# First attention: its dense pieces dealt out in halves, three quarters of the second projection taken into the last steps

## What is computed

```python
h = rmsnorm(x, attn_pre_g)
q_n, kc, vc, ksl, vsl, kwn, vwn, g_n, q_s, k_s, v_s = split(h @ w_in)
k_cmp, v_cmp = compress_kv(kc, ...), compress_kv(vc, ...)
gates = sigmoid(g_n)
# 8 heads: softmax over compressed, selected and window keys, summed by gates
o_nsa = nsa_attention(q_n, k_cmp, v_cmp, ksl, vsl, kwn, vwn, gates)
# 8 heads: softmax over a window of 128 keys, with sinks
o_swa = swa_attention(q_s, k_s, v_s, sinks)
mix = concatenate([o_nsa, o_swa]) @ w_o
x = x + rmsnorm(mix, attn_post_g)
```

## Time and profile before

| | us |
|---|---|
| median of three runs | 1287.24 (1286.85 to 1287.76) |
| the profiled execution | 1286.42 |
| its span, first to last instruction | 1284.5 |
| TensorE busy | 1263.0 |
| VectorE busy | 786.6 |
| ScalarE busy | 647.9 |
| GpSimd busy | 216.9 |

### The profile page before, as it was taken

How to read it: one execution, slowest core, us unless ns; L and a number is a source line. 1 busy time by engine, 2 the same in 40 slices (tenths; PEclk the granted TensorE clock), 3 DMA queues, 4 the chain that set the end, 5 groups by cost and what they waited for, 6 DMA issues and landing times.

```text
span 1284.5 us, 16448 instructions
## 1 busy us (share of the span) xinstructions
PE 1263.0 (98%) x6004; PEld 1045.6 (81%) x6004; DVE 786.6 (61%) x1465; ACT 647.9 (50%) x1261; POOL 216.9 (17%) x234
## 2 busy tenths in 40 slices
PE   9999999999999999999999999999999999999998
PEld 8887888878888888888787777887888888888887
DVE  6689687686645565356788876589644343343334
ACT  6787788554335433233555655586533252332344
POOL 0064555000100011001002101032311030110111
PEclk9998999999999999999999999999999999999999
DMA  7211110423333323332333212432333324233332
GB/s 275 86 50 34 42 41 26 170 82 99 90 100 98 98 90 99 99 96 68 115 91 98 76 56 68 131 112 68 98 99 92 97 75 118 79 115 89 100 90 67
DMA packets 64626, 118.20 MB, mean 92 GB/s; under 512 B 7713, under 2 KB 12193, under 8 KB 64289
## 3 DMA queue, kind: packets, MB, share of 16 engines
q1 hardware_dynamic: 62704, 112.86, 29.3%
q10 hardware_dynamic: 1840, 4.29, 1.1%
HBM read 115.02 MB, written 2.10 MB: 91 GB/s over the span
## 4 chain that ended last, share of the span: by engine, by line
PE 90%; DVE 4%; ACT 2%; issue 2%; DMA 1%; POOL 1%; POOLq 0%; SPq 0%; DVEq 0%; ACTq 0%
PE bank L593 26%; PE bank L595 25%; PE bank L594 25%; PE bank L813 2%; PE bank L693 2%; PE bank L694 2%; PE bank L695 2%; PE bank L826 1%; PE bank L827 1%; PE bank L799 1%; PE bank L800 1%; PE bank L767 1%; DVE q2p L2191 0%; DMA praw<-in_pT 0%; DVE r_bc L2086 0%
## 5 line engine op out<-in xcount | busy, mean ns | idle before, releaser
L2022 DVE TENSOR_TENSOR wl<-raw,wh 128x512 fp32r<-128x512 f32 (+2 forms) x360 | 267.5, 754 | 325.5 <-ACT wh L1323 324.8
L1323 ACT ACTIVATE wh<-raw 128x512 fp32r<-128x512 f32 (+1 forms) x398 | 242.2, 618 | 284.7 <-PE bank L595 273.7
L593 PE MATMUL bank<-AH,wh 128*128 128x512 f32 (+1 forms) x848 | 333.8, 394 | 2.1 <-DVE AL L2036 0.8
L595 PE MATMUL bank<-AH,wl 128*128 128x512 f32 (+1 forms) x848 | 329.3, 388 | 0.0
L594 PE MATMUL bank<-AL,wh 128*128 128x512 f32 (+1 forms) x848 | 327.0, 386 | 0.0
L593 PE MATMUL bank<-BH,wh 128*128 128x512 f32 x624 | 247.7, 397 | 1.6 <-ACT acc L1533 1.6
L595 PE MATMUL bank<-BH,wl 128*128 128x512 f32 x624 | 244.6, 392 | 0.0
L594 PE MATMUL bank<-BL,wh 128*128 128x512 f32 x624 | 243.0, 389 | 0.0
L595 PEld LDWEIGHTS bank<-AH,wl 128*128 128x128 f32 x848 | 159.6, 188 | 35.8
L593 PEld LDWEIGHTS bank<-AH,wh 128*128 128x128 f32 x848 | 159.9, 189 | 35.2 <-issue 2.9
L594 PEld LDWEIGHTS bank<-AL,wh 128*128 128x128 f32 x848 | 159.7, 188 | 33.0 <-issue 0.2
(11 more groups left out here) (332 smaller groups left out, 1617.4 us busy)
## 6 DMA issues: line engine op xcount, KB each, us to landing
raw<-in_w_dn SPq DMA_DIRECT2D x104, 256.0 KB, 2.7
raw<-in_w_gu SPq DMA_DIRECT2D x88, 256.0 KB, 2.6
raw<-in_w_up SPq DMA_DIRECT2D x64, 256.0 KB, 2.6
raw<-in_w_nsa SPq DMA_DIRECT2D x16, 256.0 KB, 2.7
raw<-in_w_pg SPq DMA_DIRECT2D x16, 256.0 KB, 2.7
raw<-in_w_naq SPq DMA_DIRECT2D x16, 256.0 KB, 2.7
nbi<-in_na_bias ACTq DMA_DIRECT2D x8, 448.0 KB, 3.4
raw<-in_w_swa SPq DMA_DIRECT2D x10, 256.0 KB, 2.7
```

Of the source, the lines that this page charges most:

```text
L593: t.matmul(o, w, xh, start=start, stop=False, skip_group_check=skip)
L595: return t.matmul(o, wl, xh, start=False, stop=stop, skip_group_check=skip)
L1323: a.activation(W[i % NW].h[:, 0:n], RAW[i % NRAW][:, 0:n], ACT.Copy).then_inc(*s_wh.up(i))
L2022: v.tensor_tensor(w.l[:, 0:n], RAW[i % NRAW][:, 0:n], w.h[:, 0:n], ALU.subtract).then_inc(*s_wl.up(i))
```

## The change

- `PARTS1` takes the place of `FILL1` and gives each piece by step with the halves to do there: `ALL` (four chunks), `FRONT` (the first two), `BACK` (the last two). A piece in two halves keeps its bank from one step to the next. `FILL1` is made from it with the step of the second half, and the other engines' loops read that. The order of the pieces changes for `w_nsa` 14 and 15, which now come ahead of the `w_o_swa` pieces.
- Step 7, empty before, gets `w_nsa` 3 (second half of the `wn` keys), and `w_nsa` 10 to 12 move a step ahead each. Steps 11 to 15 have a half each, steps 16 to 27 one or two halves, none is empty.
- The first three chunks of `w_o_nsa` 0, 1 and 2 (`out_front`) are done in steps 28, 29 and 30, ahead of the values of the step; those of piece 3 behind the loop; then the last chunk of all four (`out_back`), and `product` for pieces 4 to 7.
- The second attention's `behind_last` is spelt with the same two functions, for two pieces.

```diff
-FILL1 = {0: [("w_swa", 6), ("w_swa", 7)], 1: [("w_swa", 8)], 2: [("w_nsa", 0), ("w_swa", 9)], 3: [("w_nsa", 1)],
-         4: [("w_nsa", 8)], 5: [("w_nsa", 9)], 6: [("w_nsa", 2)], 8: [("w_nsa", 3)], 9: [("w_nsa", 10)],
-         10: [("w_nsa", 11)], 11: [("w_nsa", 12)], 12: [("w_nsa", 13)], 13: [("w_o_swa", 0)],
-         14: [("w_o_swa", 1), ("w_o_swa", 2)], 15: [("w_nsa", 14)], 16: [("w_nsa", 15)], 18: [("w_o_swa", 3)],
-         21: [("w_o_swa", 4)], 23: [("w_o_swa", 5)], 26: [("w_o_swa", 6)], 27: [("w_o_swa", 7)]}
+ALL, FRONT, BACK = (0, 1), (0,), (1,)
+PARTS1 = {0: [("w_swa", 6, ALL), ("w_swa", 7, ALL)], 1: [("w_swa", 8, ALL)], 2: [("w_nsa", 0, ALL), ("w_swa", 9, ALL)],
+          3: [("w_nsa", 1, ALL)], 4: [("w_nsa", 8, ALL)], 5: [("w_nsa", 9, ALL)], 6: [("w_nsa", 2, ALL)], 7: [("w_nsa", 3, ALL)],
+          8: [("w_nsa", 10, ALL)], 9: [("w_nsa", 11, ALL)], 10: [("w_nsa", 12, ALL)], 11: [("w_nsa", 13, FRONT)],
+          12: [("w_nsa", 13, BACK)], 13: [("w_nsa", 14, FRONT)], 14: [("w_nsa", 14, BACK)], 15: [("w_nsa", 15, FRONT)],
+          16: [("w_nsa", 15, BACK), ("w_o_swa", 0, FRONT)], 17: [("w_o_swa", 0, BACK), ("w_o_swa", 1, FRONT)],
+          18: [("w_o_swa", 1, BACK)], 19: [("w_o_swa", 2, FRONT)], 20: [("w_o_swa", 2, BACK), ("w_o_swa", 3, FRONT)],
+          21: [("w_o_swa", 3, BACK)], 22: [("w_o_swa", 4, ALL)], 23: [("w_o_swa", 5, FRONT)], 24: [("w_o_swa", 5, BACK)],
+          25: [("w_o_swa", 6, ALL)], 26: [("w_o_swa", 7, FRONT)], 27: [("w_o_swa", 7, BACK)]}
+FILL1 = {s: [(name, i) for name, i, h in parts if 1 in h] for s, parts in PARTS1.items()}
...
-            def part(name, k, src, ready, ks, key, first, last, between=None):
-
-                if first:
+            def part(name, k, src, ready, ks, key, first, last, between=None, halves=ALL):
+
+                if first and 0 in halves:
                     b, free = bank.take(key)
                     e.wait_ge(*free)
...
-                for j in range(4):
+                for j in range(2 * halves[0], 2 * halves[-1] + 2):
...
+            def out_front(name, c, src, ready, key):
+
+                b, free = bank.take((key, c))
+                w, i = weights(name, c)
+                e.wait_ge(*free)
+                for k in range(3):
+                    e.wait_ge(ready(k))
+                    col = slice(P * k, P * k + P)
+                    triple(b[:, :], w.h[:, col], src[k].h, src[k].l, w.l[:, col], k == 0, False)
+
+            def out_back(name, c, src, ready, key):
+
+                w, i = weights(name, c)
+                e.wait_ge(ready(3))
+                col = slice(3 * P, 4 * P)
+                m = triple(bank.ap((key, c))[:, :], w.h[:, col], src[3].h, src[3].l, w.l[:, col], False, True)
+                m.then_inc(*s_mm.up(("o", (key, c)), ("p", i)))
+                bank.give((key, c))
...
+                if s >= N_UNITS:
+                    out_front("w_o_nsa", s - N_UNITS, B, nsa_out, "wo")
                 if s >= 3:
                     values1(s - 3)
...
-            behind_last("w_o_nsa", B, nsa_out, "wo")
-            for c in range(2, 8):
+            out_front("w_o_nsa", 3, B, nsa_out, "wo")
+            for c in range(4):
+                out_back("w_o_nsa", c, B, nsa_out, "wo")
+            for c in range(4, 8):
                 product("w_o_nsa", c, B, nsa_out, [0, 1, 2, 3], 1, 4, [("wo", c)])
                 bank.give(("wo", c))
...
-            behind_last("w_out_na", A, na_out, "xo")
+            for c in range(2):
+                out_front("w_out_na", c, A, na_out, "xo")
+            for c in range(2):
+                out_back("w_out_na", c, A, na_out, "xo")
```

More of the change, by code:

```diff
@@ L888, in swa_out, with nsa_out @@
                 return [s_xl.at(("ob", "swa", k - 4))]
+            def nsa_out(k):
+                return s_xl.at(("ob", "nsa", k))
+            def out_front(name, c, src, ready, key):
[13 more added lines that the diff above has]
+                bank.give((key, c))
             scores1(0)
@@ L896, in tensor @@
                     give_turned(s - 3)
-                for name, i in FILL1.get(s, ()):
+                for name, i, halves in PARTS1.get(s, ()):
                     key, n = fill_info(name, i)
                     if name == "w_o_swa":
-                        part(name, i, B, swa_out, [4, 5, 6, 7], key, True, True)
+                        part(name, i, B, swa_out, [4, 5, 6, 7], key, True, True, None, halves)
                     else:
                         part(name, i, A, x0s, [4 * n, 4 * n + 1, 4 * n + 2, 4 * n + 3], key, n == 0, n == 1,
-                             (lambda j, kv=HIDDEN[name, i]: hidden_quarter(kv, j)) if (name, i) in HIDDEN else None)
-                    if n == 1:
+                             (lambda j, kv=HIDDEN[name, i]: hidden_quarter(kv, j)) if (name, i) in HIDDEN else None, halves)
+                    if n == 1 and 1 in halves:
                         later.append(key)
```

## The result

| | us |
|---|---|
| before, median of four runs beside it | 1287.05 (1286.27 to 1287.76) |
| after, median of four runs | 1297.56 (1296.78 to 1298.44) |
| ratio | 1.0082, 95% interval 1.0067 to 1.0097 |
| the profiled execution of after | 1297.04, span 1295.2 |

The change makes the kernel 10.5 us slower. That is outside the predicted range. In the changed kernel the lines have moved: dense matmuls L598 to L600 (before L593 to L595), turn L818, `cmp` scores L848, values L831 and L832, squares L729 (before L724), copy of a `w_o_swa` result L1547 (before L1533), adding of a closing output L2228 (before L2214), its low part L2233 (before L2219), normalisation L2983.

What follows compares the result with a forecast made beforehand. TensorE, busy 98%, was taken as the bound. Losses of 13.7 us before became 14.4 with a clock fall in step 9 or 12.8 without, weighed to +0.3 on 1287.24: 1287.5 us, range 1283.5 to 1291.5.

Steps and rivals of the forecast that it cites:

- Four weight pieces instead of two are held; the fifth is ready ... Nothing: After the loop, second projection: holding four weight pieces was to cost nothing, as the sixth is needed 5.5 us later.
- Part 1, step 7: Piece put into empty step 7: its turn no longer waits, 2.2 us won, and the clock need not fall at 103.2.
- the 3.4 us put down for the clock: Half clock from 103.2 to 110 us in the kernel before: 3.4 us lost, to be won back.
- the exchange in step 9: Step 9: 1.8 us of waits ahead of the scores go; a 3.0 us wait behind VectorE's key parts and add comes.
- The walk of the banks: Following which PSUM bank came free when, in both versions, to find where TensorE would wait for a bank.
- The add of step 9: VectorE's L2214, expected to end at 117.4 us, after TensorE arrived at 114.4, and so to release step 9's 3.0 us wait.
- Part 1, clock and small waits: Clock falls in step 9, three times in four, costing up to 3.4 us; small waits after: 0.5 with it, 2.3 without.
- Part 2: Steps 10 to 21 in halves: 3.4 us won at steps 14, 24, 27; waits 1.4 in step 19, 2.4 in 22.
- The fall of the clock that a rival placed in step 28 or 22: Slower rival: second clock fall in step 28 or 22, 3.4 us each; 1291 for one, 1294 for both; chance 0.33.
- Part 3, waits: Second projection in steps 28 to 30: waits 0.6 in step 27, 2.0 in 28, 0.95 after the loop; step 29's covered.
- the forecast without a fall in step 9: Sum of waits if the clock holds in step 9: 12.8 us against 13.7 before, that is -0.9 us.
- The rule on VectorE and GpSimd: SBUF exclusion of VectorE and GpSimd: step 9's wait nearer 4.3 than 3.0 us, total 1.3 later; not in the sum.

Runs made afterwards that it cites:

- e5: Kernel before with only SP's queue reordered: `praw` first, second `w_ple` piece behind the second `X` piece; 1286.71 us, ratio 0.9994.
- e3: Changed kernel with only SP's queue reordered: `praw` first, second `w_ple` piece behind the second `X` piece; 1290.82 us.
- e6: Kernel before with the pieces of steps 8 to 12 one step earlier, filling step 7 and emptying step 12; 1286.75 us, ratio 0.9997.
- e8: As e7, but `w_o_swa` 6 in halves in steps 24 and 26, 7 in halves in 26 and 27; 1286.79 us, ratio 0.9997.
- e9: Changed kernel with only `praw` moved ahead of the `X` pieces on SP's queue; 1295.62 us.
- e11: As e7, with one front of `w_o_nsa` added in step 29; 1285.74 us, ratio 0.9989 to the kernel before.
- e4: Changed kernel with the fronts of steps 28 to 30 behind the step's values, not ahead; 1295.65 us, ratio 1.0068 to the kernel before.
- e7: Changed kernel's halves to step 20, later `w_o_swa` pieces reordered, e3's queue, no fronts in steps 28 to 30; 1285.34 us, ratio 0.9987 to before.
- e10: Changed kernel with only the second `w_ple` piece moved behind the second `X` piece on SP's queue; 1296.82 us.
- e2: Kernel before, pieces whole and in their old steps, plus only the three fronts in steps 28 to 30; 1296.23 us, ratio 1.0074.

## Why the prediction was wrong, by its own steps

- **Part 3, "Four weight pieces instead of two are held; the fifth is ready ... Nothing".** This is the step that failed. It priced the banks, the weight buffers and output 3, and ended at the last dense matmul. It followed the transfers of the moved pieces themselves, not the two waits that SP's queue makes on TensorE's values of unit 27 and on VectorE's third add. Three fronts of 2.06 us stand ahead of these values and a fourth behind them, ahead of output 3's last chunks; the third add's lead went from 12.8 to 9.0 us and the room from 11.0 to 7.15. All needed rows were in the trace of before: SP's issues from 228.55 us on, and ScalarE's waits of 2.68 us for `praw` and 0.72 us for `w_ple`, the sign that nothing was to spare. It cost 8.1 of the 10.7 us between the two traces.
- **Part 1, step 7.** Right: no wait, full clock, 2.2 us of start-to-start time gone. But the 3.4 us put down for the clock were too many: by the traces of before and e5 (the section on the hardware) about 2, an estimate.
- **Part 1, the exchange in step 9.** Right in size, wrong in place and cause. The 3.0 us (3.0 start to start, 2.82 idle) stand one step earlier, in step 8, at the turn's second bank, which is last held by the compressed values (`vc`). ScalarE's four key copies, at 107.03 to 109.61 us, now come ahead of its copy of `vc` (110.16) and VectorE's part ends at 111.98. The walk of the banks shows it: in the kernel before that bank went to the scores of the same step, two operations later. I had followed the bank of step 9 only. The add of step 9, which the prediction named, makes TensorE wait 0.7 us more. The expectations of the runs still call this wait step 9's, and its cause the key parts; it is ScalarE's key copies and step 8.
- **Part 1, clock and small waits.** The forecast let the clock fall there three times in four, and it didn't in the profiled execution (of the ten traces with this wait it fell in five, so three in four was high); without it 2.3 us of small waits were expected up to step 14. Measured, start to start: 0.7 (step 9), 0.9 (11), 1.6 (12) and 0.6 (14), together 3.8 us, 1.5 more.
- **Part 2.** Steps 19 and 22 as priced: 1.46 (1.4) and 2.40 us (2.4). Step 24 0.18 (0.15). The fall of the clock that a rival placed in step 28 or 22 came in 22, and cost 1.6 us, not 3.4: 3.4 is its length, at half speed.
- **Part 3, waits.** Step 27 0.9 (0.6), step 28 1.6 (2.0), behind the loop 0.9 (0.95). Step 29 has 0.65 us that was not foreseen: the front of step 29 takes a bank whose output VectorE adds (L2228) only then.
- **The sum.** Up to the last dense matmul the forecast without a fall in step 9 was -0.9, measured +2.6. The difference of 3.5 is, within 0.2, the clock of step 22 (1.6), steps 9 to 14 (1.5), step 29 (0.65) and steps 27 and 28 (-0.1). This part alone would have ended at 1289.8 us, within the range; e1, which has the halves without the fronts, took 1289.2, and its trace loses 2.4 us up to the last dense matmul, counted from just ahead of step 7.
- **The rule on VectorE and GpSimd.** It was given 1.3 us at the wait of 3.0 us and had no part there. It shows one step later. Of the four low parts of the keys in after, the first three took 0.69 to 0.78 us, the first two beside GpSimd's normalisation, and the fourth 1.68 us beside its low part of a weight:

```profile
112.01 0.72 DVE L2118 TENSOR_TENSOR kb_wn<-tmp,ka_wn 64x512 fp32r<-64x512 f32 x1
...
114.25 1.68 DVE L2119 TENSOR_TENSOR kb_wn<-tmp,ka_wn 64x512 fp32r<-64x512 f32 x1
```

```profile
112.18 1.52 POOL L2983 TENSOR_SCALAR pp<-pp,small,ones 128x256 f32<-128x256 f32 x1
113.67 1.72 POOL L2957 TENSOR_TENSOR wl<-raw,wh 128x512 fp32r<-128x512 f32 x1
```

The fourth is 1.0 us longer, and it stands in front of the add that step 9 waits 0.7 us for. The Trainium skill, SBUF — State Buffer, section "Who interferes with whom", gives a lock for both GpSimd instructions, as both read SBUF; the trace agrees for L2957 alone.

## What to carry to other kernels

When work is moved ahead of a point, list every queue that waits for that point, the transfer queue first, and for each what is issued behind the wait and how much work is left between that wait and the user. A queue in fixed order passes a delay on to transfers that don't depend on it: here two moved lines on SP's queue were worth 6.7 us. A short wait of TensorE (0.2 us here) behind other engines that wait for transfers themselves is an edge and not a reserve.

## What the runs showed of the hardware that was not expected

**The clock's fall is not a property of the kernel.** after and e3 have the same program on TensorE up to the end of the attention, and the same waits in step 8 (2.82 and 2.83 us) and step 22 (2.25 in both). In after the clock held behind the one of step 8 and fell behind the one of step 22; in e3 it was the reverse, and there it fell a second time, behind the 1.4 us wait of step 12 that after has too. The windows of e3:

```profile
112.70:116.20 3.50, 3.50 (x19) 3.41 (x18) 3.44 (x4) 0.61 (x2) 2.99 (x2) 0.64 0.00 0
138.00:141.50 3.50, 3.50 (x14) 2.81 (x15) 3.40 (x8) 1.68 (x5) 1.52 (x3) 0.57 0.00 0
189.90:193.90 4.00, 4.00 (x24) 3.44 (x24) 1.93 (x5) 3.14 (x10) 1.96 (x4) 1.00 0.23 66
```

Ten traces have the 2.8 us wait of step 8: the clock fell there in e3, e6, e8, e9 and e11 and held in after, e1, e4, e7 and e10. Of the six with the 2.25 us wait of step 22 it fell in after, e1, e4 and e9 and held in e3 and e10. The Trainium skill, TensorE: Matmul & The Clock Gate, Part 1, says of a kernel's start that the number of slow matmuls varies from run to run; these traces show such a spread in the middle of a kernel. So a single trace can't tell whether a wait "costs a fall", only that it can. The same holds for the kernel before: over 33 runs its mean clock was 0.998 in 11 of them and 0.995 in 7.

**A fall costs little where VectorE is the bound.** From the first matmul of step 7 to the `cmp` scores of step 12 after took 35.4 us (100.02 to 135.39, no fall) and e3 35.4 us (100.30 to 135.71, with 3.4 us at half clock): nothing lost, as the small waits behind it vanish. From step 22 to the turn of step 24, where VectorE is less busy, after took 14.3 us (188.44 to 202.75, with a fall) and e3 12.7 (189.90 to 202.62, without): all 1.6 us lost. e3's second fall lies between: from the `cmp` scores of step 12 to the dense matmul of step 19 after took 35.5 us (135.39 to 170.93) and e3 36.7 (135.71 to 172.39), 1.1 us for 3.4 us at half clock. The fall at 103 us can be priced by e5, which is the kernel before up to SP's queue at the end: there it lasted 3.4 us and not 6.8, and from the turn of step 7 to the dense matmul that waits in step 14 e5 took 44.1 us (102.55 to 146.68) and before 45.2 (101.04 to 146.21). So 3.4 us more of half clock, 1.7 us of work, cost 1.0 us, and all 6.8 some 2 us by this estimate, where the prediction took 3.4. In the kernel before, the seven runs at 0.995 took 1288.2 us in the mean and the eleven at 0.998 1286.5; where their clock fell is not on record, and in e5's and e1's traces one fall each lies far behind the attention (871 and 768 us), so this is no price of the fall at 103 us. That VectorE is the bound there is read from its 44.3 us busy of 46 in after; it wasn't tried by taking work from it, and stays an inference.

**The same transfer takes 6.6 to 8.3 us.** The second `w_ple` piece, 256 KB, is issued behind the same four transfers in the kernel before, e1, e2, e4 and after. From its issue to ScalarE's use it took 6.7, 6.6, 6.6, 7.0 and 8.3 us. With e2's time after's wait at the squares would have been 4.2 us, which is what e2 shows (from 252.45 to 256.63). What makes one execution's transfer slower was not tried and stays open. Where the room is short, this spread is the kernel's own.
